# A 1-core transformer kernel: small loads at the start reordered, side work moved between matmuls, all conv projections in merged rows

## The chip, the cores and the metric

One core of a Trainium2 chip. The time is the device time of one execution in microseconds; of several runs the median is taken. The core has five engines: TensorE (PE, matmuls; PEld is its loading of weights), VectorE (DVE), ScalarE (ACT), GpSimd (POOL) and SyncE (SP). They run on their own and meet at semaphores. Loads are issued by SP, ACT and POOL. Matmul results stand in PSUM, which has eight banks of 512 float32 columns.

## The reference, cut to what matters

256 rows of width 1024 go through two layers of a first block and one of a second: mixer, cross attention to 256 memory rows, MLP with squared ReLU; then a final norm and a block with two more kinds of attention and an MLP. Everything is float32. The mixer of the second layer is the part whose projections the change rewrites:

```python
def odd_mixer(h, w_in, conv_w, w_out):
    S = h.shape[1]
    proj = h @ w_in                       # 1024 x 3072
    b_gate = proj[..., :CONV_DIM]
    c_gate = proj[..., CONV_DIM:2 * CONV_DIM]
    z = c_gate * proj[..., 2 * CONV_DIM:]
    zp = jnp.pad(z, ((0, 0), (CONV_WIDTH - 1, 0), (0, 0)))
    y = zp[:, 0:S] * conv_w[0]
    for tap in range(1, CONV_WIDTH):
        y = y + zp[:, tap:tap + S] * conv_w[tap]
    return (b_gate * y) @ w_out
```

The first layer's mixer is a differential attention with a bias by distance (from a small table) and a factor `lam` (exponentials of two dot products), beside a pooling over windows. The cross attention is softmax(q k) v over 4 heads of 256.

## The kernel before

**Units and halves.** All weights come as one stream of units of 1024 x 512 (`UNITS`, in the order of `SECTIONS`), each in two halves of 1 MB. A half goes through a ring of four places: SP loads it to `raw` (L1117), ACT makes its high part `hi` (`hi_half`, L1176), DVE the low part `lo` = raw − hi (`lo_half`, L1699), and PE multiplies. A product in float32 is made of three: x_hi·w_hi, x_hi·w_lo and x_lo·w_hi. `refill(u, b)` on ACT and DVE makes the half that stands four places behind (u, b); ACT does so once PE has used (u, b). SP loads a half into its place when the low part of the one before is made.

**Four ways to do a unit.** `unit_w` (L496) holds weights in the array and streams 256 columns of x, three matmuls for each of 4 column groups and 8 chunks: 96 matmuls into two banks. `unit_m` (L509, L516) holds the same weights but streams x_hi and x_lo side by side, 512 columns, with w_hi (`upper`), and then x_hi alone, 256 columns, with w_lo (`lower`): 32 + 32 matmuls into four banks. The two halves of a bank must then be added: ACT copies the second half out (`low_parts`, L1212), DVE adds the first to it (`sums`, L1746) and the bank is free. Half 0 of a unit runs upper, lower; half 1 lower, upper. `unit_x` and `pair` (L544) hold rows of x and stream 512 columns of weights, 12 matmuls for each tile and half.

**Conv.** Six units: for each half of the channels c_gate, the other factor of z, and b_gate. Units 0 and 3 are `unit_m`, the other four `unit_w` in banks 4, 5 or 6, 7. DVE multiplies gate and z out of the banks into `z_pad` (L2165), makes twelve taps (L2176, L2178), multiplies by b_gate (L2186) and splits the result into `yt_hi` and `yt_lo`; `conv_out`, a `pair`, uses the two halves of yt.

**Hooks.** Side work of PE (scores, transposes, probabilities times values) is called from inside a unit: `hooks[b, j]` ahead of a column group j of half b, `(t, b)` or `(t, b, k)` ahead of a chunk k in `unit_x`. In `cross`, the scores of heads 0 and 1 (L820), the transposes of their softmax (`turns`, L830) and the product with the values (L841) stand in the second query unit. In `mlp` with `by_tile` the first hidden tiles are squared by DVE (L2041) and turned by PE (`hidden_turned`, L878). In `fq`, `forget_turned` (L938) and `forget_sums` (L946 to L948) stand in the second tile.

**The start.** PE does `first_unit` (l0_u) chunk by chunk, `bias_rows` (a product of the bias table, L650), then l0_q, l0_k, l0_v. ACT copies the bias row (L1279), sums squares, and waits for `lam_sums` before it goes on; DVE waits for the loads of `cols` and `lam` (L1813) and makes those sums. POOL first waits until the bias row is read, then issues its stores and loads: `row_dram`, `cols`, `lam_in`, `mem`. The bias row goes to DRAM, is written there expanded (`rows_dram`, L2448), read back shifted into `bias1` and `bias0` and masked (L2462, L2464); DVE uses it in the logits (L1866).

The order on each engine is the order in which the program is written.

Of the kernel before, what the change touches and what calls it, by code (L numbers as in the profile page):

```python
# [11 lines left out]
ALU = mybir.AluOpType  # L12
# [9 lines left out]
HC = KC // 2  # L22
# [158 lines left out]
def program(nc, ctx, d, out):  # L181
# [225 lines left out]
    def fill(label):  # L407

        return fills[label][1]
# [19 lines left out]
    for _u in range(NU):  # L429
        name = NAME[_u]  # L430
        if (name in ("q0", "q1")
                or (name == "conv" and (_u - UNIT["conv"]) % 3 == 0)
                or (name in ("mlp0", "mlp1", "mlp2") and (_u - UNIT[name]) % 4 < 2
                    and (int(name[3]), (_u - UNIT[name]) // 4, (_u - UNIT[name]) % 4) not in BY_TILE)):
            MERGED.append(_u)
# [8 lines left out]
    def _(pe):  # L444
# [58 lines left out]
        def unit_m(u, x, banks, waits=((), ()), hooks={}):  # L503

            def upper(b, j):
                if b == 0:
                    claim(banks[j], ("u", u, j))
                for k in range(HC):
                    mm = pe.matmul(ps[:, banks[j], :], hi[:, POS[(u, b)] % RING, k, j * P:(j + 1) * P],  # L509
                                   flat(x[2][:, b * HC + k]), start=(b == 0 and k == 0),  # L510
                                   stop=(b == 1 and k == HC - 1), skip_group_check=True)
                return mm

            def lower(b, j):
                for k in range(HC):
                    mm = pe.matmul(ps[:, banks[j], 0:S], lo[:, POS[(u, b)] % RING, k, j * P:(j + 1) * P],  # L516
                                   x[0][:, b * HC + k, :], start=False, stop=False, skip_group_check=True)
                return mm

            for b, parts in ((0, (upper, lower)), (1, (lower, upper))):  # L520
                for part in parts:
                    for j in range(4):
                        if part is parts[0]:
                            if j == 0:
                                need(u, b)
                                wait_all(waits[b])
                        if part is parts[j // 2] and (b, j) in hooks:
                            hooks[b, j]()
                        mm = part(b, j)
                        if b == 1 and part is upper and j < 3:  # L530
                            filled_by(mm, ("u", u, j))
                used(mm, u, b, ("u", u, 3) if b else None)
# [88 lines left out]
        def split(n):  # L621

            return ((read((n, 0, 0)), read((n, 1, 0))), (read((n, 0, 1)), read((n, 1, 1))))
# [182 lines left out]
        def cross(x):  # L806
# [39 lines left out]
            def both(f, a, b):  # L846
                def run():
                    f(a)
                    f(b)
                return run  # L850

            unit_m(u, XT, (2, 3, 0, 1), split(x))
            unit_m(u + 1, XT, (2, 3, 0, 1), hooks={(0, 2): both(scores, 0, 1), (1, 1): both(turns, 0, 1),
                                                   (1, 3): both(values, 0, 1)})
            scores(2)

# [13 lines left out]
        def mlp(m, n, by_tile=False, late={}):  # L870

            u0 = UNIT[f"mlp{m}"]

            def hidden_turned(t):
                pe.wait_ge(*hid_sq.at((m, 0, 0, t)))
                o = claim(4 + t, ("hid", m, t))
                for k in range(HC):
                    mm = pe.transpose(o[:, k * P:(k + 1) * P], hn[:, t, k * P:(k + 1) * P], ident[:, :])  # L878
                filled_by(mm, ("hid", m, t))

            for j in range(4):
                u = u0 + 4 * j
                w0, w1 = ((hid_ready.at((m, j, c)),) if (m, j, c) not in BY_TILE else None for c in range(2))
                if j == 0 and by_tile:
                    second = ({(0, 1, 3): lambda: transposes_by_half(n, 1)} if m == 2 else
                              {(0, 1, 2): lambda: transposes(n, 1)})
                    transposes_late = {**second, (1, 1): lambda: hidden_turned(0)}
                    unit_x(u, XT, (0, 1), n, transposes_late)
                    unit_m(u + 1, XT, (2, 3, 6, 7), hooks={(0, 1): lambda: hidden_turned(1)})
                    w0 = (read(("hid", m, 0)), read(("hid", m, 1)))  # L890
                elif j == 0:
                    unit_m(u, XT, range(4, 8), split(n))
                    unit_m(u + 1, XT, range(4, 8))
                else:
                    unit_m(u, XT, range(4, 8))
                    unit_m(u + 1, XT, range(4, 8))
                pair(u + 2, (w0, w1), late if j == 3 else {}, first=(j == 0), last=(j == 3))
# [12 lines left out]
        mlp(0, "mlp0")  # L910
        filler_x("kv1c", "mix1")
        for n in range(6):
            if n % 3 == 0:
                unit_m(UNIT["conv"] + n, XT, (2, 3, 0, 1), split("mix1") if n == 0 else ((), ()),
                       {(1, 0): mod_turn(0, 7)} if n == 3 else {})
            else:
                unit_w(UNIT["conv"] + n, XT, (4, 5) if n % 3 == 1 else (6, 7))
        pair(UNIT["conv_out"], ((yt_ready.at(("conv", 0)),), (yt_ready.at(("conv", 1)),)))
        filler_x("kv1d", "x1")

# [26 lines left out]
            pe.matmul(o[:, 8:16], tri_m[:, P - 1:P].to_broadcast((P, P)), lf0, start=True, stop=False, skip_group_check=True)  # L947
            filled_by(pe.matmul(o[:, 8:16], tri_m, lf1, start=False, stop=True, skip_group_check=True), "cum")  # L948

        unit_x(UNIT["fq"], XT, (2, 3), hooks={(1, 0): forget_turned, (1, 1): forget_sums})  # L950

        def aug_turned(x, src, t, b):

# [175 lines left out]
    def _(act):  # L1129
# [145 lines left out]
                first_hi((c + 1) // 2)  # L1275
        for k in range(2, RING):
            hi_half(k)
        act.wait_ge(*fill("bias_row"))
        act.activation(bias_row[0:4, :], bank("bias_row")[0:4, 0:384], ACT.Copy).then_inc(*free("bias_row"))  # L1279
        act.dma_start(gain, d["gains"][1:2, :].to_broadcast((P, D))).then_inc(loaded["gain_mem"], 16)  # L1280
        for t in range(T):
            act.wait_ge(loaded[f"x{t}"], 16)
# [2 lines left out]
        act.wait_ge(loaded["ident"], 16)  # L1285
        for pad in (ff_hi, ff_lo):
            act.activation(pad[:, 64:], ident[:, 0:120], ACT.Copy).then_inc(pad_set, 1)
        act.wait_ge(*lam_sums.at(1))
        for n in range(2):
            act.activation(lam[:, 2 + n:3 + n], lam[:, n:n + 1], ACT.Exp).then_inc(*lam_exp.up(n))  # L1290
# [7 lines left out]
        for t in range(T):  # L1298
            for b in range(2):
                sum_squares("mem", t, b, mem_rows[:, t, :])  # L1300
        stream(UNIT["l0_k"])
        for b in range(2):
            act.wait_ge(*fill(("pool_t", b)))
            act.activation(pool_t[:, 2 * b:2 * b + 2, :], cut(bank(("pool_t", b)), 2), ACT.Copy)\
                .then_inc(*free(("pool_t", b)))
# [172 lines left out]
        for b in range(2):  # L1478
            u = UNIT["conv"] + 3 * b
            if b == 0:  # L1480
                act.wait_ge(ada_used, 8)
            else:
                act.wait_ge(*conv_z.at(0))
            keep_low(u, gate_c)
            if b == 1:
                mod_kept(0)
            stream(u + 1)
            stream(u + 2)
            split_hi(("conv", b), yt_hi[:, 4 * b:4 * b + 4, :], conv_y, *conv_y_ready.at(b))
        boundary("x1", UNIT["conv_out"], UNIT["kv1d"], kv_v[:, 0, NB:D])  # L1490
        cross("x1")
# [160 lines left out]
    def _(dve):  # L1652
# [503 lines left out]
        for b in range(2):  # L2156
            u = UNIT["conv"] + 3 * b
            keep_sums(u, gate_c)
            for n in range(4):
                dve.wait_ge(*read(("u", u, n)))  # L2160
            refill(u + 1, 0)
            for n in range(2):
                label = ("u", u + 1, n)
                dve.wait_ge(*fill(label))
                dve.tensor_tensor(z_pad[:, 2 * n:2 * n + 2, 2:], gate_c[:, 2 * n:2 * n + 2, :],  # L2165
                                  cut(bank(label), 2), ALU.mult).then_inc(*free(label))
            for n in range(2):
                dve.wait_ge(*read(("u", u + 1, n)))
            dve.engine_nop().then_inc(*conv_z.up(b))
            refill(u + 1, 1)  # L2170
            for tap in range(3):
                for c in range(4):
# [6 lines left out]
                                                       ALU.add)  # L2179
                    step(ins, wait=(c == 3))  # L2180
            refill(u + 2, 0)
            for n in range(2):
                label = ("u", u + 2, n)
                dve.wait_ge(*fill(label))
                y = conv_y[:, 2 * n:2 * n + 2, :]
                dve.tensor_tensor(y, y, cut(bank(label), 2), ALU.mult).then_inc(*free(label))  # L2186
            for n in range(2):
                dve.wait_ge(*read(("u", u + 2, n)))
            dve.engine_nop().then_inc(*conv_y_ready.up(b))
            split_lo(("conv", b), (slice(None), slice(4 * b, 4 * b + 4), slice(None)), conv_y)  # L2190
            refill(u + 2, 1)
        boundary("x1", UNIT["conv_out"], UNIT["kv1d"], kv_v[:, 1, NB:D])
# [219 lines left out]
    def _(gp):  # L2412
# [23 lines left out]
            gp.wait_ge(*normed.at((last, T - 1)))  # L2436
            load_gain(n)

        gp.wait_ge(*read("bias_row"))
        gp.dma_start(row_dram, bias_row[0:4, :]).then_inc(bias_stored, 16)  # L2440
        gp.dma_start(cols[:, :], d["cols"]).then_inc(loaded["consts"], 16)
        gp.dma_start(lam_in, d["lam"].to_broadcast((P, 4, 64))).then_inc(loaded["lam"], 16)
        for t in range(T):
            gp.dma_start(mem_rows[:, t, :], d["mem"][t * P:(t + 1) * P, :]).then_inc(loaded["mem"], 16)
        roots("mix0")
        gp.wait_ge(bias_stored, 16)
        copies = bass.AP(tensor=row_dram.tensor, offset=0, ap=[[384, 4], [0, P], [1, 384]])
# [171 lines left out]
```

## Time and profile before

| | us |
|---|---|
| median of 3 runs (lowest, highest) | 1090.54 (1088.89, 1091.45) |
| profiled execution | 1090.96 |
| its span | 1089.1 |
| busy: PE, PEld | 1077.3 (99%), 931.6 (86%) |
| busy: DVE, ACT, POOL | 729.4 (67%), 521.9 (48%), 63.8 (6%) |
| loaded from DRAM | 223 MB, 207 GB/s with what is written |

Times in the profile are microseconds from the start of the span. Matmuls are pipelined: the duration of one (392 ns for 512 columns) overlaps the next, and the ends are modelled, so lengths of stretches say more than sums of durations. "Idle before" is the time in which an engine had nothing to run, with what released it.

### The profile page before, as it was taken

Reading aid. Unit: us, or ns where it says so; the run is one execution under the profiler, and the core shown is the slowest. Engines: PE = TensorE matmul, PEld = TensorE weight load, DVE = VectorE, ACT = ScalarE, POOL = GpSimd, SP = SyncE. Lnnn points to the kernel's source line nnn. Section 1 sums busy time; section 2 is a strip of 40 time slices with the busy share of each in tenths; the row PEclk is TensorE's granted clock in tenths of the full one; section 3 lists DMA queues with packets and bytes.
Section 4 is the critical chain, followed back from the end, with each engine's and each line's share of the span. In section 5 each row is a group of like instructions: output and inputs, shape, how many; then the busy total and the mean of one; then the engine's idle time right before and its main releaser. Section 6 shows DMA issues by size and latency. Waiting matters only on the chain.

```text
span 1089.1 us, 14074 instructions
## 1 busy us (share of the span) xinstructions
PE 1077.3 (99%) x5867; PEld 931.6 (86%) x5867; DVE 729.4 (67%) x789; ACT 521.9 (48%) x598; POOL 63.8 (6%) x111
## 2 busy tenths in 40 slices
PE   9899999999999999999999999999999999999998
PEld 8888898898888888998887888888788887888886
DVE  4767565477878676766646777869767488574654
ACT  5555555354534445344545353544565465453441
POOL 1201000000000000000001000000201010000000
PEclk9999999999999999999999999999999999999999
DMA  9934563466786746554545778674334473655531
GB/s 367 343 142 174 193 213 116 174 213 251 269 331 219 297 158 220 189 192 162 205 150 207 275 261 333 215 301 182 120 144 165 152 253 119 227 194 193 193 116 39
DMA packets 33071, 225.16 MB, mean 207 GB/s; under 512 B 4288, under 2 KB 4484, under 8 KB 8560
## 3 DMA queue, kind: packets, MB, share of 16 engines
q1 hardware_dynamic: 26784, 187.97, 47.0%
q0 software_dynamic: 5824, 35.64, 9.1%
q8 instruction: 47, 0.77, 0.3%
q10 hardware_dynamic: 400, 0.64, 0.2%
q14 instruction: 16, 0.13, 0.0%
HBM read 223.16 MB, written 1.87 MB: 207 GB/s over the span
## 4 chain that ended last, share of the span: by engine, by line
PE 95%; DVE 2%; ACT 1%; DMA 1%; issue 0%; POOL 0%; ACTq 0%; DVEq 0%
PE ps L544 48%; PE ps L509 19%; PE ps L496 10%; PE ps L516 10%; PE ps L820 1%; PE ps L841 1%; PE ps L676 1%; PE ps L605 1%; DMA work<-in_lam 1%; DVE lo L1699 1%; PE ps L984 0%; PE ps L1030 0%; PE ps L686 0%; PE ps L615 0%; ACT hi L1176 0%
## 5 line engine op out<-in xcount | busy, mean ns | idle before, releaser
L1699 DVE TENSOR_TENSOR lo<-raw,hi 128x2048 fp32r<-128x2048 f32 x158 | 360.9, 2288 | 154.7 <-ACT hi L1176 154.5
L1176 ACT ACTIVATE hi<-raw 128x2048 fp32r<-128x2048 f32 x158 | 302.1, 1914 | 249.0 <-PE ps L544 142.0
L544 PE MATMUL ps<-hi,yt_hi 128*128 128x512 f32 x544 | 213.4, 392 | 0.0
L509 PE MATMUL ps<-xt,hi 128*128 128x512 f32 x896 | 212.4, 391 | 0.0
L544 PE MATMUL ps<-hi,yt_lo 128*128 128x512 f32 x544 | 211.7, 389 | 0.0
L544 PE MATMUL ps<-lo,yt_hi 128*128 128x512 f32 x544 | 211.7, 389 | 0.0
L509 PEld LDWEIGHTS ps<-xt,hi 128*128 128x128 f32 x896 | 166.1, 188 | 33.1
L544 PEld LDWEIGHTS ps<-hi,yt_lo 128*128 128x128 f32 x544 | 102.1, 188 | 21.2
L544 PEld LDWEIGHTS ps<-lo,yt_hi 128*128 128x128 f32 x544 | 102.2, 188 | 20.9
L544 PEld LDWEIGHTS ps<-hi,yt_hi 128*128 128x128 f32 x544 | 102.2, 188 | 20.9
L544 PE MATMUL ps<-hi,xt 128*128 128x512 f32 x352 | 117.6, 400 | 0.1
L516 PEld LDWEIGHTS ps<-xt,lo 128*128 128x128 f32 x896 | 111.6, 191 | 2.3
L516 PE MATMUL ps<-xt,lo 128*128 128x256 f32 x896 | 113.1, 283 | 0.0
L544 PEld LDWEIGHTS ps<-hi,xt 128*128 128x128 f32 x352 | 65.9, 188 | 14.5 <-DVE xt L1787 0.9
L496 PE MATMUL ps<-xt,hi 128*128 128x256 f32 x384 | 71.6, 287 | 2.8 <-DVE lo L1699 2.8
L544 PE MATMUL ps<-lo,xt 128*128 128x512 f32 x176 | 68.7, 390 | 0.0
L2103 DVE CUSTOM_DVE_ANT_0 work<-work 128x1024 f32<-128x1024 f32 x48 | 56.2, 1220 | 15.0 <-DMA work<-in_w_ada 15.0
L496 PEld LDWEIGHTS ps<-xt,hi 128*128 128x128 f32 x384 | 61.5, 196 | 3.8 <-DVE lo L1699 3.7
L1212 ACT ACTIVATE hn<-ps 128x512 f32<-128x512 f32 x44 | 26.3, 598 | 67.5 <-PE ps L509 67.5
L496 PE MATMUL ps<-xt,lo 128*128 128x256 f32 x192 | 55.0, 287 | 0.0
L496 PE MATMUL ps<-mt,hi 128*128 128x256 f32 x256 | 49.5, 287 | 0.0
L1746 DVE TENSOR_TENSOR hn<-ps,hn 128x256 f32<-128x256 f32 x88 | 33.0, 419 | 24.2 <-ACT hn L1212 21.4
(280 smaller groups left out, 1099.8 us busy)
## 6 DMA issues: line engine op xcount, KB each, us to landing
raw<-in_weights SPq DMA_DIRECT2D x174, 1024.0 KB, 4.9
work<-in_w_ada POOLq DMA_DIRECT2D x16, 1536.0 KB, 7.7
work<-in_gains POOLq DMA_DIRECT2D x6, 512.0 KB, 4.1
work<-mod_rows POOLq DMA_DIRECT2D x6, 512.0 KB, 5.5
raw<-in_weights SPq DMA_DIRECT2D x4, 512.0 KB, 7.5
h<-in_x SPq DMA_DIRECT2D x2, 512.0 KB, 4.3
work<-in_pool SPq DMA_DIRECT2D x1, 1024.0 KB, 9.8
work<-in_mem POOLq DMA_DIRECT2D x2, 512.0 KB, 10.7
```

The source lines that it names most:

```text
L496: mm = pe.matmul(o, ws[:, slot, k, j * P:(j + 1) * P], xs[:, c, :], start=(c == 0 and n == 0 and j % 2 == 0), stop=(c == KC - 1 and n == 2 ...
L509: mm = pe.matmul(ps[:, banks[j], :], hi[:, POS[(u, b)] % RING, k, j * P:(j + 1) * P], flat(x[2][:, b * HC + k]), start=(b == 0 and k == 0) ...
L516: mm = pe.matmul(ps[:, banks[j], 0:S], lo[:, POS[(u, b)] % RING, k, j * P:(j + 1) * P], x[0][:, b * HC + k, :], start=False, stop=False, s ...
L544: mm = pe.matmul(ps[:, n, :], xs[:, c, t * P:(t + 1) * P], ws[:, slot, k, :], start=(first and k == 0 and i == 0), stop=(last and k == HC ...
L605: mm = pe.transpose(o[:, k * P:(k + 1) * P], hn[:, t, c * P:(c + 1) * P], ident[:, :])
L676: mm = pe.matmul(ps[:, t, :], xs[:, c, t * P:(t + 1) * P], ws[:, POS[(u, b)], k, :], start=(c == 0 and i == 0), stop=(c == KC - 1 and i == 2),
L820: mm = pe.matmul(o[:, t * S:(t + 1) * S], cq_t[:, c, t * P:(t + 1) * P], keys(c), start=(dc == 0), stop=(dc == 1), skip_group_check=True)
L1176: act.activation(hi[:, p % RING], raw[:, p % RING], ACT.Copy).then_inc(hi_ready, 1)
L1212: act.activation(dst[:, 2 * n:2 * n + 2, :], ps[:, b0:b0 + 2, S:NB], ACT.Copy)\
L1699: dve.tensor_tensor(lo[:, p % RING], raw[:, p % RING], hi[:, p % RING].bitcast(F32), ALU.subtract)\
L1746: dve.tensor_tensor(dst[:, n, :], bank(label)[:, 0:S], dst[:, n, :], ALU.add).then_inc(*free(label))
L2103: ins = dve.tensor_tensor_reduce(ada[:, n, :], ada[:, n, :], c_act, 1.0, 0.0, ALU.mult, ALU.add, mod[:, c:c + 1])
```

## The change

- POOL waits for the last chunk of the first unit's weights instead of the bias row, loads `cols`, `lam_in` and `mem`, and only then waits for the bias row and stores it.
- ACT copies the bias row after the gain load, the four sums of squares and the two pads, and has one more wait, for the stored row, ahead of `pool_t` (the two lie in the same place).
- `unit_m` runs its hooks ahead of `upper` groups only. The hooks of `cross`, `mlp` and `fq` get new places.
- All six conv units are `unit_m`, in banks (2, 3, 0, 1) and (4, 5, 6, 7) by turns. `z` and `y` are made from sums in SBUF: ACT copies the low halves to `z_pad` and `gate_c`, DVE adds and multiplies. `mod_turn` is put in bank 3.

```diff
-                or (name == "conv" and (_u - UNIT["conv"]) % 3 == 0)
+                or name == "conv"
...
-                        if part is parts[j // 2] and (b, j) in hooks:
+                        if part is upper and (b, j) in hooks:
                             hooks[b, j]()
...
-            unit_m(u + 1, XT, (2, 3, 0, 1), hooks={(0, 2): both(scores, 0, 1), (1, 1): both(turns, 0, 1),
+            unit_m(u + 1, XT, (2, 3, 0, 1), hooks={(0, 3): both(scores, 0, 1), (1, 0): both(turns, 0, 1),
                                                    (1, 3): both(values, 0, 1)})
...
-                    transposes_late = {**second, (1, 1): lambda: hidden_turned(0)}
+                    transposes_late = {**second, (1, 1, 2) if m == 2 else (1, 1): lambda: hidden_turned(0)}
                     unit_x(u, XT, (0, 1), n, transposes_late)
-                    unit_m(u + 1, XT, (2, 3, 6, 7), hooks={(0, 1): lambda: hidden_turned(1)})
+                    unit_m(u + 1, XT, (2, 3, 6, 7), hooks={(0, 2): lambda: hidden_turned(1)})
...
-            if n % 3 == 0:
-                unit_m(UNIT["conv"] + n, XT, (2, 3, 0, 1), split("mix1") if n == 0 else ((), ()),
-                       {(1, 0): mod_turn(0, 7)} if n == 3 else {})
-            else:
-                unit_w(UNIT["conv"] + n, XT, (4, 5) if n % 3 == 1 else (6, 7))
+            unit_m(UNIT["conv"] + n, XT, (2, 3, 0, 1) if n % 2 == 0 else range(4, 8),
+                   split("mix1") if n == 0 else ((), ()), {(1, 0): mod_turn(0, 3)} if n == 3 else {})
...
-        unit_x(UNIT["fq"], XT, (2, 3), hooks={(1, 0): forget_turned, (1, 1): forget_sums})
+        unit_x(UNIT["fq"], XT, (2, 3), hooks={(1, 0, 1): forget_turned, (1, 1): forget_sums})
...
-        act.wait_ge(*fill("bias_row"))
-        act.activation(bias_row[0:4, :], bank("bias_row")[0:4, 0:384], ACT.Copy).then_inc(*free("bias_row"))
         act.dma_start(gain, d["gains"][1:2, :].to_broadcast((P, D))).then_inc(loaded["gain_mem"], 16)
...
             act.activation(pad[:, 64:], ident[:, 0:120], ACT.Copy).then_inc(pad_set, 1)
+        act.wait_ge(*fill("bias_row"))
+        act.activation(bias_row[0:4, :], bank("bias_row")[0:4, 0:384], ACT.Copy).then_inc(*free("bias_row"))
         act.wait_ge(*lam_sums.at(1))
...
         stream(UNIT["l0_k"])
+        act.wait_ge(bias_stored, 16)
...
-                act.wait_ge(*conv_z.at(0))
+                act.wait_ge(*conv_y_ready.at(0))
             keep_low(u, gate_c)
             if b == 1:
                 mod_kept(0)
-            stream(u + 1)
-            stream(u + 2)
+            keep_low(u + 1, z_pad[:, :, 2:])
+            act.wait_ge(*conv_z.at(b))
+            keep_low(u + 2, gate_c)
...
+            z = z_pad[:, :, 2:]
             refill(u + 1, 0)
-            for n in range(2):
-                label = ("u", u + 1, n)
-                dve.wait_ge(*fill(label))
-                dve.tensor_tensor(z_pad[:, 2 * n:2 * n + 2, 2:], gate_c[:, 2 * n:2 * n + 2, :],
-                                  cut(bank(label), 2), ALU.mult).then_inc(*free(label))
-            for n in range(2):
+            sums(u + 1, z)
+            for n in range(4):
                 dve.wait_ge(*read(("u", u + 1, n)))
-            dve.engine_nop().then_inc(*conv_z.up(b))
+            dve.tensor_tensor(z, z, gate_c, ALU.mult).then_inc(*conv_z.up(b))
+            dve.wait_ge(*conv_z.at(b))
             refill(u + 1, 1)
...
             refill(u + 2, 0)
-            for n in range(2):
-                label = ("u", u + 2, n)
-                dve.wait_ge(*fill(label))
-                y = conv_y[:, 2 * n:2 * n + 2, :]
-                dve.tensor_tensor(y, y, cut(bank(label), 2), ALU.mult).then_inc(*free(label))
-            for n in range(2):
+            sums(u + 2, gate_c)
+            for n in range(4):
                 dve.wait_ge(*read(("u", u + 2, n)))
-            dve.engine_nop().then_inc(*conv_y_ready.up(b))
+            dve.tensor_tensor(conv_y, conv_y, gate_c, ALU.mult).then_inc(*conv_y_ready.up(b))
+            dve.wait_ge(*conv_y_ready.at(b))
...
-        gp.wait_ge(*read("bias_row"))
-        gp.dma_start(row_dram, bias_row[0:4, :]).then_inc(bias_stored, 16)
+        gp.wait_ge(chunk_landed[HC - 1], 16)
         gp.dma_start(cols[:, :], d["cols"]).then_inc(loaded["consts"], 16)
         gp.dma_start(lam_in, d["lam"].to_broadcast((P, 4, 64))).then_inc(loaded["lam"], 16)
         for t in range(T):
             gp.dma_start(mem_rows[:, t, :], d["mem"][t * P:(t + 1) * P, :]).then_inc(loaded["mem"], 16)
+        gp.wait_ge(*read("bias_row"))
+        gp.dma_start(row_dram, bias_row[0:4, :]).then_inc(bias_stored, 16)
```

## Rows read from the trace of the kernel before

**Rows 1.** The page's totals: engine, busy us (share of the span), instructions.
```profile
PE 1077.3 (99%) x5867; PEld 931.6 (86%) x5867; DVE 729.4 (67%) x789; ACT 521.9 (48%) x598; POOL 63.8 (6%) x111
```

**Rows 2.** PE's waits: line, releaser: us in total, times, longest.
```profile
PE ps L496 <- DVE lo L1699: 2.8, 1, 2.8
PE ps L878 <- DVE hn L2041: 1.8, 3, 0.8
```

**Rows 3.** Stretches at the start: from:to, us, busy by engine, PEclk, DMA, GB/s.
```profile
32.96:35.79 2.83, 0.01 (x2) 0.00 (x1) 2.35 (x2) 2.83 (x4) 0.00 (x0) 1.00 0.63 216
35.79:40.40 4.61, 4.61 (x26) 4.61 (x27) 4.61 (x3) 4.08 (x3) 0.00 (x0) 0.63 0.83 291
40.40:49.49 9.09, 9.09 (x79) 9.09 (x78) 7.47 (x7) 4.75 (x10) 5.84 (x7) 1.00 0.97 363
```

**Rows 4.** The chain that ended last, at the start: start us, us, what.
```profile
23.36 7.39 DMA work<-in_lam
33.44 2.30 DVE lo L1699
```

**Rows 5.** Timeline of ACT, DVE and POOL at the start: start, us, engine, line, operation.
```profile
13.21 1.17 ACT L1147 ACTIVATE hi<-raw 128x512 fp32r<-128x512 f32 x2
16.72 1.92 ACT L1176 ACTIVATE hi<-raw 128x2048 fp32r<-128x2048 f32 x1 [0.53 <-DMA raw<-in_weights]
18.67 2.29 DVE L1699 TENSOR_TENSOR lo<-raw,hi 128x2048 fp32r<-128x2048 f32 x1 [0.16 <-ACT hi L1176]
22.07 0.72 POOL L2440 DMA_DIRECT2D bias_row_store<-work  x1 [21.11 <-ACT work L1279]
```

**Rows 6.** Stretches: conv unit 0, conv units 1 and 2, q0's second unit.
```profile
417.58:428.69 11.11, 11.11 (x66) 9.84 (x66) 7.74 (x9) 4.43 (x3) 0.00 (x0) 1.00 0.63 228
428.69:451.73 23.04, 23.04 (x194) 23.04 (x193) 15.99 (x21) 8.15 (x5) 0.00 (x0) 1.00 0.51 180
166.09:186.04 19.95, 19.34 (x106) 16.79 (x105) 9.89 (x16) 10.29 (x17) 0.00 (x0) 1.00 0.43 156
```

**Rows 7.** DVE's timeline in conv: last two sums, eight taps, the half products.
```profile
429.42 0.76 DVE L1746 TENSOR_TENSOR work<-ps,work 128x256 f32<-128x256 f32 x2 [1.06 <-ACT work L1212]
445.63 3.38 DVE L2178 SCALAR_TENSOR_TENSOR work<-work,cols 128x256 f32<-128x256 f32 x8
451.26 1.27 DVE L2186 TENSOR_TENSOR work<-work,ps 128x512 f32<-128x512 f32 x2
```

**Rows 8.** The chain in q0's second unit: scores, probabilities, column groups.
```profile
170.69 3.47 PE ps L820 x16
176.16 0.63 DVE hn L2066 x2
177.49 1.43 PE ps L516 x12
```

**Rows 9.** The chain at the hidden turns of mlp1 and mlp2.
```profile
591.31 0.44 PE ps L878 x4
595.93 0.66 PE ps L878 x4
915.78 0.66 PE ps L878 x4
```

**Rows 10.** PE's timeline ahead of mlp2's first turn and at the forget gate.
```profile
914.60 0.39 PE L544 MATMUL ps<-hi,xt 128*128 128x512 f32 x1
782.52 0.39 PE L544 MATMUL ps<-hi,xt 128*128 128x512 f32 x1
783.13 0.28 PE L938 MATMUL ps<-ident,late 8*128 8x8 f32 x2 [0.22 <-DVE late L2286]
```

**Rows 11.** Timeline of POOL and DVE: the last mask and the first logits.
```profile
57.70 0.63 POOL L2464 TENSOR_SCALAR_AFFINE_SELECT work<-work 128x512 f32<-128x512 f32 x1
66.66 0.87 DVE L1866 SCALAR_TENSOR_TENSOR hn<-ps,q_scale,work 128x256 f32<-128x256 f32 x2
```

## Prediction

> **What bounds the kernel now.** First the engine totals: TensorE (PE) is busy for 1077.3 us of 1089.1, DVE for 67%, the others for less [rows 1]. So the span is the length of PE's instruction stream, and an edit is worth what it takes out of that: instructions, waits, time at the lower clock. Work on DVE, ACT and the queues counts only where PE ends up waiting for it. Second, PE's waits: the longest, 2.8 us, is in the start; the next group is that for DVE's squares in the MLPs [rows 2], and two more kinds stand at hooks that this change moves. A wait costs more than it shows, since the end of the last matmul is modelled and what follows a wait isn't overlapped yet; so each is priced from stretches and pieces of the chain.
>
> **1. The start.** The stretches [rows 3]: l0_q ends at 32.96, PE stands for 2.83 us, and in the 4.61 us behind it the granted clock is 0.63 of full speed, mostly the lower level, 1.2 instead of 2.4 GHz; from 40.40 it is 1.00. The chain through it [rows 4]: the small load in_lam is issued at 23.36 and lands at 30.75; DVE sums it, ACT takes its exponentials and only then makes the high part of l0_k's first weights; DVE makes their low part from 33.44, PE goes on at 35.79. in_lam is late because its issue stands on POOL behind the store of the bias row, which goes out at 22.07, after PE has done l0_u [rows 5]. After the change POOL waits for the last chunk of the first weights instead. ACT uses this chunk at 13.21 [rows 5], so in_lam is issued about 12 to 14, and with its 7.4 us lands at 20 to 22. DVE is free from 20.96, ACT from 18.64 [rows 5]; four squares (2.5 us) and about 1.2 us of pads and bias copy take ACT to 22.4, exponentials and high part to 24.4, the low part (2.3) is done at 26.7, or at 29 with in_lam 2 us late. PE wants it at 32.96: cover 4 to 6 us. What else moves: mem rows, cols and the gain row now compete with the weight halves 3 to 5. The DMA engines move up to 0.4 MB per us here [rows 3], so 1.2 MB can delay a half by 3 us at most; l0_q's second half is wanted at 27, its low part is there at 20.96. ACT's bias copy behind the squares and pads delays the bias chain by 1 us (rival A); the mix0 roots on POOL, now behind the same store, start no later than before. Worth: 2.83 for the wait, and for the slow clock: l0_k takes 4.61 + 9.09 = 13.70 us [rows 3], less 0.44 for the key scales (four matmuls, as in rows 9) is 13.26, against 11.52 (half of 23.04, [rows 6]) at full clock: 1.74. Together **4.6 us**; bounds 0 (something as late takes its place) and 4.6.
>
> The Trainium skill's "DMA: Bandwidth & Descriptors", section "Issuing engines are not separate DMA queues", speaks against this part: loads from all engines run on the same 16 DMA engines and interleave, so an earlier load is paid for by the others. By it the sum stays only as long as the 3 us above fit the cover; rivals A and D are the cases in which they don't.
>
> **2. Conv units.** Four of six change from 96 matmuls of 256 columns to 32 of 512 and 32 of 256. Two of the old kind take 23.04 us, in which the weight loads (PEld) are busy all the time; one of the new kind takes 11.11 with PEld busy for 9.84 [rows 6]. The same columns stream, 32 weight loads less are made. 2 × (23.04 − 22.22) = **1.6 us**, measured on both forms in this very section; bounds 1.5 and 1.7.
>
> The Trainium skill's "TensorE: Matmul & The Clock Gate", section "Back-to-back issue gap", gives N/2.4 + 2.5 ns for an isolated matmul at full clock; by it the part would bring 0.3 us (96 × 109.2 = 10.48 us a unit against 32 × 215.8 + 32 × 109.2 = 10.40). The rows differ.
>
> Price elsewhere: per channel half DVE does eight sums (0.76 for two) and two whole products (1.25 each) where it did four half products (1.27 for two) [rows 7], that is 3.0 + 2.5 in place of 2.5: 3.0 us more, on 23.7 busy of 34.2 [rows 6]. ACT gets four copies of 0.6. By hand from a unit's end E: ACT's copy and the last two sums to E+1.5 [rows 7], product 2.8, low part 5.1, twelve taps (eight take 3.38 [rows 7]) 10.2, low part 12.5, sums of the next unit 14.0, product 15.3, ACT's split 16.3, DVE's 17.5. A set of banks is claimed again 11.1 us after its unit's end and is free 2.9 after it (14.0 − 11.1). yt is ready 6.4 after the last unit; conv_out wants it after 48 matmuls, 10.9. Cover 4.5. The new waits (ACT for conv_z ahead of the next keep_low, DVE for its own products) stand inside this chain, and behind them are only weight halves wanted a unit later. mod_turn in bank 3, free by then, costs PE what it did in bank 7.
>
> **3. Cross attention, twice.** The scores move ahead of the last 512-column group, the turns behind all 256-column groups of the second half. In q0 the unit with its hooks takes 19.95 us [rows 6]. Without waits: 11.11, scores and values at 3.47 each, two turns at 0.44: 18.93. Why [rows 8]: scores end at 174.16, reduce, exponential and product are done at 176.79, and PE has 12 matmuls (1.43) and one turn for these 2.7 us. After: 4 of 0.228 and 32 of 0.12, 4.7 us. The scores come 1.9 us earlier, 2.7 after the unit's start; they need the unit before evicted, 1.5 after its end by [rows 7]. The values keep 2.7 us behind the turns for two ACT copies of 0.6. q1 repeats it. 2 × 1.02 = **2.0 us**, bounds 1.6 and 2.1.
>
> **4. Hidden turns.** In mlp1 the last tile ends at 591.75 + 2.74 = 594.5; four matmuls (0.91) later PE wants DVE's square, which is ready at 595.93. Until the turn ends there are 2.09 us where 0.91 + 0.44 are work [rows 9]: 0.7. With eight matmuls (1.82) it is covered by 0.4. mlp2 has the same (the third wait of [rows 2]): 0.7; and its turn 0, wanted at 914.60 + 0.23 = 914.83, starts at 915.78 [rows 9, 10]: 1.0 with the slower restart, covered by six matmuls (1.37). Together **2.4 us**, bounds 1.8 and 2.5.
>
> **5. Forget gate.** Wanted at 782.52 + 0.23 = 782.75, started at 783.13 [rows 10]: **0.4**; three matmuls (0.68) cover it. The sums behind it keep nine matmuls, 2.0 us, for one small copy.
>
> **Sum.** 4.6 + 1.6 + 2.0 + 2.4 + 0.4 = 11.0 us. The profiled execution took 1090.96 us (span 1089.1, 1.9 around it): 1079.9. It lay 0.4 above the median of the runs shown, 1090.54: forecast 1079.5.
>
> **Rivals.**
> A. Something takes part of the start's place. The candidate is the bias chain: row store, expanded write, gather and mask, all on POOL's queue. It ends at 58.33, and DVE needs it for the logits at 66.66 [rows 11]; with PE 4.6 us earlier that is 62.1, cover 3.7. For it: the store goes behind 1.2 MB of loads in the same queue, 1 us later. Against it: mem, which it went ahead of, no longer stands before the expanded write. Behind the logits the softmax steps pass between DVE and ACT one by one, so I take a late mask as paid one to one. 1 to 4 us: 1080.5 to 1083.5. Chance 0.15.
> B. A chain in conv or behind a moved hook is longer than the rows show (DVE has 3.0 us more per half) and 1.5 to 3.5 of the 6.4 us of parts 2 to 5 aren't had: 1081 to 1083. Chance 0.13.
> C. The step depends on columns alone and the busy PEld in [rows 6] is no bound: both forms stream 24576 columns, part 2 brings nothing, 1081.1. Against it: both forms stand timed in [rows 6]. Chance 0.02. The Trainium skill's formula in part 2 is nearly this case.
> D. POOL's loads aren't served while SP's queue is full, and in_lam lands near 30 as before: 4.6 us stay, 1084.1. For it: 7.4 us for so small a load [rows 4]. Chance 0.05.
> E. Slower: the same starvation holds the bias chain. DVE stops at the mask, with the low parts of kv0's second block behind it, and PE behind those. To eat 11.0 us it must stop PE for 9.3 (a fall of the clock, as in [rows 3], adds 1.7), so it decides from a mask at 71.4 on, 13 us later than now: 1091 to 1094. Against it: 58.33 was reached with the queue as full. Chance 0.03.
>
> **How the numbers follow.** The forecast has 0.62, with 1078.0 to 1080.5. Upward the range takes in B, C and most of A: 1083.0; D and E are left out, and some of A. A measurement of this kernel tells about 0.2%, 2.2 us, from no change; all cases but E lie further off, and E is shared with a bit of no change: faster 0.95, same 0.02, slower 0.03.
>
> **What would show it.** Right: no wait for L1699 near 33 and no clock under 1.00 near 36; a conv unit 11.1 us; q0's and q1's second unit 18.9; no waits at L830 and L938, and at L878 under 0.1. Wrong: in_lam landing after 27; a wait at l0_k's first weights or at a diff turn; conv_out waiting for yt.

## Result and the profile after

The changed kernel takes 1083.08 us (median of 4 runs, 1082.11 to 1084.38) beside 1090.59 for the kernel before: a ratio of 0.9934, 95% interval 0.9916 to 0.9952 (ratios here are estimated over all runs and not from the two medians). It is faster by 7.5 us where 11.0 were forecast, and stands just above the upper end of the range, 1083.0. Its runs come in two groups: 1082.11 and 1082.19 with a mean granted clock of 1.000, and 1083.96 and 1084.38 with 0.998. The profiled execution is of the first group: 1082.11 us, span 1080.3 against 1089.1. Of all runs here one, in e2, was slow (2652.52 us, granted clock 1.000); it is in none of the medians.

The page after, its totals (the line that answers to [rows 1]) and the first group of matmuls with an idle time that the page before doesn't have:

```profile
PE 1072.4 (99%) x5739; PEld 922.9 (85%) x5739; DVE 735.2 (68%) x801; ACT 527.2 (49%) x606; POOL 67.9 (6%) x111
...
L509 PE MATMUL ps<-xt,hi 128*128 128x512 f32 x1024 | 243.3, 391 | 1.8 <-ACT work L1254 1.8
```

PE has 128 instructions less (four units of 96 matmuls became four of 64). DVE has 12 more and 5.8 us more work; 3.0 for each of the two channel halves were forecast. PE's list of waits, which answers to [rows 2]:

```profile
PE ps L509 <- ACT work L1254: 1.8, 1, 1.8
PE ps L686 <- DVE late L1802: 1.2, 1, 1.2
PE ps L676 <- DVE lo L1666: 0.9, 1, 0.9
```

All the waits that the change aimed at are gone: l0_k's first weights, the hidden turns, the probabilities, the forget gate. q0's second unit takes 18.95 us, where 18.93 were forecast. The one at the top is new. L1254 of the changed kernel is ACT's copy of the modulation columns out of bank 3 (`mod_kept`). The other two belong to the first microseconds and are no part of the change.

The start, in the chain (start us, us, what): l0_q and l0_k run through, where [rows 3] had 2.83 us of idle and 4.61 us at 0.63 of the clock.

```profile
20.53 0.73 PE ps L650 x2
21.26 14.59 PE ps L496 x120
35.85 0.45 PE ps L694 x4
36.30 8.63 PE ps L496 x72
```

Conv, in the chain of the same execution:

```profile
437.87 3.83 PE ps L516 x32
441.70 7.28 PE ps L509 x32
448.98 3.83 PE ps L516 x32
452.81 0.11 PE ps L643
452.92 3.67 PE ps L509 x16
...
457.17 1.90 ACT hi L1173
459.07 0.16 ACT work L1254
...
459.27 3.02 PE ps L509 x12
462.29 3.83 PE ps L516 x32
```

Each unit is 3.64 + 3.83 + 3.64 = 11.11 us as forecast. But unit 4, which starts at 456.59, has its first four column groups done at 462.29, 5.70 us later instead of 3.64: 2.06 us lost. It did the first group (0.91), stood for 1.79 and went on at 459.27, when ACT had done its half of 1.90 us and then the small copy. The chain says who was late: unit 4 claims banks 2, 3, 0, 1 in this order, and bank 3 still held the transposed modulation columns. PE had written them at 452.81, six microseconds before; ACT's copy stands behind `keep_low` of unit 3, whose parts wait for the end of that unit and whose last refill is a whole half.

### The profile page after: what moved, and what is told of

Read it like the earlier page. It is cut to its first block, busy times and chain, and to the rows that moved or that the text cites. A ratio compares the mean times of both kernels' runs of the same rounds, so it can differ in the third digit from the quotient of the medians.

```text
span 1080.3 us, 13851 instructions
## 1 busy us (share of the span) xinstructions
PE 1072.4 (99%) x5739; PEld 922.9 (85%) x5739; DVE 735.2 (68%) x801; ACT 527.2 (49%) x606; POOL 67.9 (6%) x111
## 4 chain that ended last, share of the span: by engine, by line
PE 99%; DMA 1%; ACT 0%; DVE 0%; issue 0%; SPq 0%; ACTq 0%
PE ps L544 50%; PE ps L509 22%; PE ps L516 11%; PE ps L496 6%; PE ps L841 1%; PE ps L820 1%; PE ps L676 1%; PE ps L605 1%; DMA raw<-in_weights 1%; PE ps L981 1%; PE ps L1027 0%; PE ps L615 0%; PE ps L960 0%; PE ps L1039 0%; PE ps L830 0%; PE ps L752 0%
## 5 line engine op out<-in xcount | busy, mean ns | idle before, releaser
L509 PE MATMUL ps<-xt,hi 128*128 128x512 f32 x1024 | 243.3, 391 | 1.8 <-ACT work L1254 1.8
L509 PEld LDWEIGHTS ps<-xt,hi 128*128 128x128 f32 x1024 | 189.7, 188 | 40.2 <-ACT work L1254 2.2
L516 PEld LDWEIGHTS ps<-xt,lo 128*128 128x128 f32 x1024 | 127.1, 192 | 2.5
L516 PE MATMUL ps<-xt,lo 128*128 128x256 f32 x1024 | 127.8, 283 | 0.0
L544 PE MATMUL ps<-hi,mt 128*128 128x512 f32 x128 | 42.3, 397 | 0.0
L496 PEld LDWEIGHTS ps<-mt,hi 128*128 128x128 f32 x256 | 40.8, 191 | 1.0 <-issue 0.7
L544 PEld LDWEIGHTS ps<-lo,xt 128*128 128x128 f32 x176 | 33.2, 188 | 6.1
```

The lines of the kernel that those rows point to most:

```text
L496: mm = pe.matmul(o, ws[:, slot, k, j * P:(j + 1) * P], xs[:, c, :], start=(c == 0 and n == 0 and j % 2 == 0), stop=(c == KC - 1 and n == 2 ...
L544: mm = pe.matmul(ps[:, n, :], xs[:, c, t * P:(t + 1) * P], ws[:, slot, k, :], start=(first and k == 0 and i == 0), stop=(last and k == HC ...
```

## Experiments

Two theories at first. **W**: what is missing is this wait at bank 3, and a fall of the clock that follows it in some runs. **S**: it is spread between runs, or the added sums and products cost time elsewhere. Each run is compared with runs of the kernel before on the same chip: 1090.65 us (9 runs) for e1 to e4, 1090.78 (16) for e5 to e8, 1091.01 (15) for e9 to e11.

### e1: the copy out of bank 3 earlier

```diff
-            keep_low(u, gate_c)
+            refill(u, 0)
             if b == 1:
                 mod_kept(0)
+            low_parts(u, gate_c)
+            refill(u, 1)
             keep_low(u + 1, z_pad[:, :, 2:])
```

> The changed kernel with one move on ACT: the copy of the turned modulation columns out of bank 3 stands ahead of the low halves of conv unit 3 instead of behind its last refill. Theory W (the wait at bank 3 and what it does to the clock are what is missing from the forecast): unit 4's first 512-column groups took 5.70 us instead of 3.64, so 2.06 us go, the profiled span is 1078.2 against 1080.3, the time 1080.0, and the two values seen in runs of the changed kernel (1082.1 and 1084.2) become one, since no idle of 1.8 us is left for the clock to fall on. Rival S (the missing time is run-to-run spread, or lies in the added sums and products): 1083 as before, with the same spread.

Measured: 1080.08 us (1080.00 to 1080.84), span 1078.3, ratio 0.9906 (0.9892 to 0.9919). One small copy in another place of ACT's order brings 3.0 us against the changed kernel's median of the result, and 4.1 against that of e3, made beside it; against the runs of the changed kernel in which the clock held (1082.1 to 1082.2) it is 2.0 to 2.1. The wait isn't in PE's list any more, and the chain in conv is unbroken:

```profile
449.06 3.83 PE ps L516 x32
452.89 0.11 PE ps L643
453.00 7.28 PE ps L509 x32
460.28 3.83 PE ps L516 x32
```

### e2: bank 1 instead of bank 3

```diff
-                   ... {(1, 0): mod_turn(0, 3)} if n == 3 else {})
+                   ... {(1, 0): mod_turn(0, 1)} if n == 3 else {})
```

> The changed kernel with the modulation transpose in bank 1 instead of 3. Bank 1 is claimed by the last group of unit 4, twelve matmuls (2.73 us) after its start, and ACT's copy is done 2.64 after it. Theory W: a wait of 0 to 0.2 us, time 1080.0 to 1080.3, no second value. Rival S: 1083.

Measured: 1080.22 to 1081.04 us (three runs), median 1080.51, ratio 0.9911 (0.9893 to 0.9929); no wait at L509. ACT copies as late as in the changed kernel; only the bank, and with it the moment at which PE asks for it, is another. So it is the order of claims and not the copy itself.

### e3: the changed kernel again

No edit.

> The changed kernel unaltered, on the same chip as the others. Theory W: each run is at 1082.2 or 1084.2, the upper ones with a mean granted clock of 0.998 and the lower ones 1.000, median between. Rival S: a spread without two levels.

Measured: 1084.16 us median (1082.12 to 1084.52), ratio 0.9936 (0.9923 to 0.9948). Two levels again: 1082.12 and 1082.16 with clock 1.000; 1084.16, 1084.45 and 1084.52 with 0.998. This profile is of an upper one. Stretches of PE behind the same wait of 1.79 us (from:to, us, busy by engine, PEclk, DMA, GB/s):

```profile
460.00:461.00 1.00, 1.00 (x4) 0.86 (x5) 1.00 (x1) 0.00 (x0) 0.56 (x1) 1.00 0.83 336
461.00:462.00 1.00, 1.00 (x4) 0.78 (x3) 1.00 (x1) 0.00 (x0) 0.00 (x0) 0.54 0.32 102
462.00:463.00 1.00, 1.00 (x4) 0.81 (x3) 0.13 (x1) 0.00 (x0) 0.00 (x0) 0.50 0.01 1
463.00:464.00 1.00, 1.00 (x4) 0.72 (x4) 0.00 (x0) 0.00 (x0) 0.00 (x0) 0.50 0.73 139
```

and its chain at the place:

```profile
459.80 0.15 ACT work L1254
...
460.00 4.61 PE ps L509 x12
464.61 3.82 PE ps L516 x32
```

The twelve matmuls behind the wait take 4.61 us where the first profile had 3.02: 1.6 us lost to the lower level, 1.2 GHz, and here the clock falls a microsecond after PE has gone on. So the same wait costs 3.7 instead of 2.1 us. The two profiled spans lie 2.3 apart; the other 0.8 is a later start (the first unit begins at 10.14 instead of 9.35). With the runs of the result that is 5 of 9 executions, counted by their mean granted clock; only two of the nine have a profile.

### e4: the wait made longer

```diff
+                act.wait_ge(*fill(("mod", 0)))
+                for i in range(6):
+                    act.activation(hn[0:24, 0, P * i:P * i + P], bank(("mod", 0))[0:24, 0:P], ACT.Copy)
                 mod_kept(0)
```

> The changed kernel with six more small ACT copies (24 x 128, 0.15 to 0.25 us each) ahead of the one that frees bank 3: PE's wait grows by 0.9 to 1.5 us to about 3. Theory W: 1083.0 to 1083.7 where the clock holds, and since the idle is as long as the 2.83 us of the start of the kernel before, it falls in most runs, which adds 1.7 to 2.0: 1085.2 on most. If the clock has nothing to do with this wait: 1083.4 in all runs. Rival S: 1083 as the changed kernel, since ACT would have room for the copies.

Measured: 1084.85 us (1084.66 to 1085.42), ratio 0.9949 (0.9935 to 0.9963), all four runs with clock 0.998. PE's wait is 2.74 us, 0.95 longer, and the matmuls behind it are slow in the profile (4.43 us for twelve). So ACT had no room at this place, which speaks against S. The fall came in all four runs, where at 1.8 us it came in 5 of 9; so few runs don't show that the longer wait made the difference. In this profile the clock falls before PE goes on, at 460.70:

```profile
460.00:461.00 1.00, 0.29 (x1) 0.30 (x2) 1.00 (x1) 0.65 (x5) 0.05 (x1) 0.67 0.57 238
```

The length of the wait alone doesn't decide. The start of the kernel before idles for 2.8 us, and 3 of the 40 runs made of it here have a mean clock of 1.000 (1088.68 to 1089.69 us). The profiles of e6 and e7 have 2.1 and 1.9 us there and the lower level behind it; that of e11 has a wait of 1.8 us elsewhere and holds 1.00.

### e5, e6, e7: each part alone on the kernel before

e5 has the new order of loads on POOL and of the bias row on ACT; e6 the moved hooks; e7 the six merged conv units, with the modulation columns in bank 3. The edits are those of the diff.

> The kernel before with the reordered start alone. By the sum of the prediction 4.6 us where the clock of the kernel before falls, as it did in 8 of 9 runs beside e1: 1086.0 to 1086.3, granted clock 1.000, no wait near 33 us. Rival A (the bias chain or a weight half takes a part): 1087 to 1089 with a wait at a diff turn or at l0_k.

> The kernel before with the hooks moved (cross, mlp, fq) and nothing else. By the sum 2.0 + 2.4 + 0.4 = 4.8 us: 1085.8, with no waits left at L830, L938 and L878. The start's wait and its clock stay. Rival B (new waits behind the moved hooks): 1087 or more.

> The kernel before with the conv part alone: six merged units, sums in SBUF, the modulation transpose in bank 3. Theory W: 1.6 us gained on the units, 2.06 lost at bank 3, so 1091.1 where the clock holds there and 1092.9 where it falls too: the part as a whole brings nothing or loses 2 us. By the prediction, without a price for bank 3: 1089.0.

| | us | against before (1090.78) | ratio, 95% | forecast |
|---|---|---|---|---|
| e5 start | 1087.01 | −3.8 | 0.9964 (0.9951 to 0.9978) | −4.6 |
| e6 hooks | 1085.78 | −5.0 | 0.9955 (0.9941 to 0.9968) | −4.8 |
| e7 conv | 1091.61 | +0.8 | 1.0006 (0.9998 to 1.0015) | −1.6 |

The hooks do what they were costed at. The conv part alone brings nothing: its 1.6 us are eaten by the wait (1.79 us in this profile too). In e7 the transpose runs earlier, 8 us ahead of ACT's copy instead of 6, since its hook still stands ahead of the 256-column groups of unit 3's second half, and the wait is the same: its length comes from ACT. By the mean clock it fell there only in 2 of the 11 runs (0.997 instead of 0.998), less often than in the changed kernel; why is open.

The start alone falls 0.8 short, which isn't clear of the noise: its interval is 2.4 to 5.3 us. Its profile has a wait that neither the kernel before nor the profile of the changed one has, at the transposes of the softmax in kv0:

```profile
PE ps L635 <- DVE hn L1886: 0.3, 1, 0.3
```

Rival A of the prediction, small. Followed back in the chain of e5 (start us, us, what):

```profile
28.43 24.63 DMA bias_rows<-bias_row_store
...
54.22 6.60 DMA work<-bias_rows
...
61.60 1.05 POOL work L2466
...
62.68 0.75 DVE work L1917
63.43 0.79 DVE hn L1867 x2
```

The mask ends at 62.65 and DVE starts at once. This profile, of the slowest of the five runs, has another 0.8 us at the very start: its first unit begins at 10.17 where the profile before has 9.35. That start moves between 9.2 and 10.2 over the 13 profiles, for one and the same kernel too (9.39 in e1 and 10.10 in e10, at 1080.06 and 1080.67 us).

### e8: mem rows late again, on e1

```diff
-        for t in range(T):
-            gp.dma_start(mem_rows[:, t, :], ...)
         gp.wait_ge(*read("bias_row"))
         gp.dma_start(row_dram, bias_row[0:4, :]).then_inc(bias_stored, 16)
+        for t in range(T):
+            gp.dma_start(mem_rows[:, t, :], ...)
```

> e1 with the two loads of mem rows put back behind the store of the bias row; cols and lam stay early. In the changed kernel the expanded bias rows landed some 25 us after their issue (18 before) and the last mask ended at 61.05, 1.1 us ahead of the first logits at 62.18, where 3.7 were forecast. If the early mem loads keep the bias rows back: mask at 57 to 59. If it is the weight stream that has no pause any more near 35 us: mask at 60 to 62. Time 1080.1 in both cases as long as the mask is in time; mem rows land near 35 and are wanted by ACT only at 36, so a delay of a few us there has cover until the transposes at 49.6.

Measured: 1080.88 us (1080.10 to 1081.72), ratio 0.9909 (0.9896 to 0.9923). The mask isn't earlier but later, 63.1, outside both cases of the expectation, and PE waits 0.9 us at L635. The expanded write takes 26.2 us (28.62 to 54.79) with mem in front of it; in the eight other profiles with the new order of loads it takes 24.5 to 24.7. So the early mem loads aren't what holds this chain back. In the four profiles that still wait at l0_k's first weights the write takes 18.0 us (before), 18.3 (e6), 19.0 (e7) and 15.3 (e9). Stretches of the kernel before and, under it, of the changed one, from 33 to 38 us:

```profile
33.00:38.00 5.00, 2.21 (x11) 2.21 (x12) 4.56 (x3) 5.00 (x6) 0.00 (x0) 0.81 0.62 205
```

```profile
33.00:38.00 5.00, 5.00 (x44) 5.00 (x44) 2.65 (x2) 4.39 (x4) 0.00 (x0) 1.00 1.02 407
```

and the two queues in the same stretch (packets, MB, share of 16 engines), before and after:

```profile
q0 software_dynamic: 731, 0.80, 44.9%
q1 hardware_dynamic: 29, 0.22, 17.2%
```

```profile
q0 software_dynamic: 246, 0.21, 12.4%
q1 hardware_dynamic: 249, 1.81, 88.8%
```

In the kernel before DVE made no low part from 20.96 to 33.44 [rows 4, 5], so SP had no place free for weights: its queue (q1) moved 0.22 MB in these 5 us instead of 1.81, and POOL's (q0) 0.80 instead of 0.21. By the sizes of the packets 0.44 of the 0.80 are the write and most of the rest is rows of mem; the 0.21 are all the write. That would fit a gap in SP's loads that the write used. But a gap alone isn't enough. From 45 to 48 of the changed kernel the DMA engines are busy for 0.37 of the time, with the write still under way:

```profile
q1 hardware_dynamic: 49, 0.29, 27.5%
q0 software_dynamic: 26, 0.12, 9.7%
```

The write goes on at the 0.04 MB per us that it had from 33 to 38. So in all 13 profiles the write is longer where the stall is gone, 24.5 us or more against 19.0 or less; by what way is open. Nor does a run here keep the stall with the new order of cols and lam, which would part the two.

### e9: conv alone, copy early

e7 with the edit of e1.

> The conv part alone on the kernel before, as in e7, with ACT's copy of the modulation columns ahead of the low halves as in e1. Theory W: the 2.06 us at bank 3 go and the 1.6 of the units is left: 1089.2 beside 1090.8 of the kernel before, e7 being at 1091.6. Rival S (the conv part costs elsewhere): 1090.8 or more.

Measured: 1088.85 us (1087.05 to 1090.25) beside 1091.01: −2.2, ratio 0.9982 (0.9974 to 0.9991). With the copy out of the way the conv part brings what the unit lengths promised (the interval is 1.0 to 2.8 us). No cost of the added sums and products shows beside the forecast 1.6, which ends S. The parts now add up, to within intervals of 1 to 2 us each: 3.8 + 5.0 + 2.2 = 11.0, and e1 has 10.6 and, again, 10.8.

### e10: e1 again

> e1 once more on another chip beside the kernel before: 1080.1 to 1080.9 in all runs, ratio 0.9905.

Measured: 1080.20 us (1080.05 to 1080.67), ratio 0.9905 (0.9891 to 0.9918). e1 beats both kernels, by 1.0% and 0.3% (e1 and e3, made side by side, are 0.4% apart).

### e11: the mask later, on e1

```diff
+        for k in range(4):
+            gp.affine_select(out=bias1[:, :, P:S], in_=bias1[:, :, P:S], ...).then_inc(set_up, 1)
+            gp.wait_ge(set_up, 5 + k)
         gp.affine_select(...
```

> e1 with the first mask done five times over instead of once on POOL (same values), 4 x 0.65 to 0.75 us more ahead of DVE's logits. In e1 the last mask ends at 61.1 and the logits start at 62.2, after a copy of 0.7 that doesn't need the mask but stands behind its wait on DVE: a cover of some 0.4 to 1.1. If a late mask is paid one to one, as rival A of the prediction took it, PE waits 1.6 to 2.4 us at the diff turns in all and the time is 1081.8 to 1082.6. If the softmax steps have room: 1080.1.

Measured: 1083.03 us (1082.97 to 1083.25), ratio 0.9930 (0.9915 to 0.9945): 2.8 us more than e10. POOL and DVE in its timeline:

```profile
63.99 0.63 POOL L2465 TENSOR_SCALAR_AFFINE_SELECT work<-work 128x512 f32<-128x512 f32 x1
64.65 0.75 DVE L1917 TENSOR_SCALAR work<-ps,rstd 128x512 f32<-128x512 f32 x1 [3.45 <-POOL work L2465]
```

and in PE's waits:

```profile
PE ps L635 <- DVE hn L1886: 1.8, 1, 1.8
PE ps L752 <- DVE hn L1867: 1.0, 1, 1.0
```

The logits' first copy starts at 64.65 instead of 61.5 to 62.2, some 2.5 to 3.1 us late, and 2.8 arrive at the end: paid one to one, as rival A had it. More than expected here, since the mask was moved by 3.5 and not 2.8 (each repeat cost a wait besides). The granted clock stays 1.00 in every microsecond of this profile from 90 to 106, though PE stands for 1.78 us until 96.53, and the four times lie within 0.3 us: the 2.8 us are the two waits and no fall.

## Why the prediction was wrong

**The step that failed** stands at the end of part 2: "mod_turn in bank 3, free by then, costs PE what it did in bank 7." It asked whether the bank was free when the transpose wanted it, and it was. It didn't ask who claims the bank next. In the kernel before bank 7 was taken next by conv unit 5, with a whole unit between; bank 3 is taken 0.91 us into the very next unit. And it didn't walk ACT's order: the copy stands behind `keep_low` of unit 3, and so comes 2.64 us after that unit's end (456.59 to 459.23). Term by term: forecast 0, measured 2.06 us where the clock held (profiled spans of e1 and the changed kernel: 2.0 apart), and another 1.6, by the chain of e3, in the 5 of 9 runs in which it fell. With the median between the two groups that is 3.0 of the 3.6 us that were missing: e1, in which this alone is mended, is at 1080.08 and 1080.20 where 1079.5 was forecast for the whole. The last 0.6 to 0.7 has no cause shown; the beginning of the first unit alone moves by 0.9 between profiles.

**The rivals.** B had the kind and the size of the bare wait, "a chain in conv or behind a moved hook" with 1.5 to 3.5 us, but named DVE's added work for it, which cost nothing (e9); and it gave no price to the clock, though the part on the start had worked out just that price, 1.74, from [rows 3]. With it B would have reached to near 1085, and the range would have held the time.

**What held.** The start: no wait, no fall of the clock, in_lam there when DVE wanted it (DVE made its sums at 21.10 without a gap). The size is open: 3.8 alone (e5, 2.4 to 5.3), after 0.3 us paid back at the diff turn, where 4.6 were forecast. Merged units: 11.11 us each. The rows were right against the page's rule for an isolated matmul, in the Trainium skill's "TensorE: Matmul & The Clock Gate", section "Back-to-back issue gap", which would have had, as an estimate, 0.3 us here; e9 has 2.2, by its interval 1.0 to 2.8. Hooks: 5.0 for 4.8, with every one of their waits gone (e6).

**Rival A**, the bias chain, was rightly seen as the next thing to be late and wrongly sized. The cover was forecast as 3.7 us. In the changed kernel the mask ends at 61.05 and DVE's logits, the line that answers to [rows 11], start at 62.18, behind a copy from 61.52 that already waits for the mask: 0.5.

```profile
60.42 0.63 POOL L2459 TENSOR_SCALAR_AFFINE_SELECT work<-work 128x512 f32<-128x512 f32 x1
61.52 0.74 DVE L1915 TENSOR_SCALAR work<-ps,rstd 128x512 f32<-128x512 f32 x1
62.18 0.86 DVE L1865 SCALAR_TENSOR_TENSOR hn<-ps,q_scale,work 128x256 f32<-128x256 f32 x2
```

The prediction took the write to be as long as before. Its argument that mem no longer stands before the write is true, and mem there does cost 1.5 us (e8, one profile), but the expanded write landed 25 us after its issue instead of 18. It did so in every profile without the stall, so removing the stall, or the new order of loads that did it, made the write slower; which, and how, isn't shown.

## What to carry to other kernels

When side work is moved to another PSUM bank, three times have to be walked: when the bank is free, when the reader empties it in its own program order, and when PE claims it next; here the last two were 1.7 us apart on the wrong side, and moving one copy of 0.25 us on ACT was worth 3 us of the median. A PE wait of about 2 us has to be priced with and without the clock behind it: 2.1 or 3.7 us here. And where a stall at the start is removed, look at the transfers that ran during it: they can be slower afterwards (18 to 25 us here), so ask whether their chain has cover left.

## What was not expected of the hardware

- The same wait of 1.79 us is followed by a fall of PE's clock to 1.2 GHz in 5 of 9 executions of one kernel (by their mean clock), and not in the others; at 2.74 us it fell in 4 of 4, at the start of the kernel before, 2.8 us, in 37 of 40; behind the 1.78 us of e11's profile it held. The fall comes 1.1 us after PE has gone on (e3), 0.3 after (before) or 0.4 ahead of it (e4), and the granted clock stays at 0.50 for 3.4 us each time. What decides isn't shown.
- POOL's DMA queue got 12% of the DMA engines' time beside a full SP queue, and 45% from 33 to 38 of the kernel before; but its write ran no faster in the changed kernel's later pause, from 45 to 48. The Trainium skill's "DMA: Bandwidth & Descriptors", section "Queues, rings and completion order", has the engines take turns between queues packet by packet. The 246 and 249 packets of the two queues in one stretch look like that, but 201 of the 246 carry 12 bytes each, and from 39 to 43 of the kernel before, with the write under way, POOL's queue has 34 packets beside 163 of SP's (0.16 and 1.24 MB). So the trace doesn't show equal turns; whether its packets are those of the page is open.
